# PEER experts: second products of four keys made in two stretches of four columns

## The reference

```python
experts = e1 * N_KEYS + e2                       # N_KEYS = 128
gate = softmax(top_s)
act = gelu(einsum('thkd,td->thk', expert_u[experts], tb)) * gate
out = einsum('thk,thkd->td', act, expert_v[experts])
```

## Time and profile before

| | us |
|---|---|
| median of 3 runs | 3780.93 (3779.2 to 3783.51) |
| the profiled execution | 3777.74 |
| its span | 3776.1 |
| TensorE matmul busy | 3400.2 (90%) |
| VectorE busy | 3066.7 (81%) |
| ScalarE busy | 1169.7 (31%) |
| GpSimd busy | 1518.2 (40%) |

### The profile page before, as it was taken

One profiled execution on the slowest core, in us unless ns is written; L12 is line 12 of the kernel. 1 busy time (PEld: TensorE's weight loads), 2 busy tenths in 40 slices (PEclk: granted clock), 3 DMA queues, 4 the chain that ended last, 5 costly groups with the idle time before them and its releaser, 6 DMA issues. The chain is left out here.

```text
span 3776.1 us, 64063 instructions
## 1 busy us (share of the span) xinstructions
PE 3400.2 (90%) x21871; PEld 3155.2 (84%) x21871; DVE 3066.7 (81%) x6071; ACT 1169.7 (31%) x2361; POOL 1518.2 (40%) x1267
## 2 busy tenths in 40 slices
PE   7998858989997998837779999999999999999997
PEld 7998747777786855537679999999999999999997
DVE  6543657676664589999879999999999999999997
ACT  3101344334232122249922222222222222222221
POOL 1120000000000023430067676676677766676772
PEclk9999769889898999969989999999999999999998
DMA  3222330010003000005499999999999999999995
GB/s 122 95 91 81 98 112 7 22 33 13 1 10 140 32 26 26 26 15 222 195 353 359 353 361 349 342 365 354 347 359 349 353 362 343 349 364 349 357 357 192
DMA packets 297939, 782.11 MB, mean 207 GB/s; under 512 B 28217, under 2 KB 130233, under 8 KB 296417
## 3 DMA queue, kind: packets, MB, share of 16 engines
q0 software_dynamic: 135568, 493.54, 35.5%
q1 hardware_dynamic: 162256, 287.15, 21.3%
HBM read 709.91 MB, written 70.11 MB: 207 GB/s over the span
## 5 line engine op out<-in xcount | busy, mean ns | idle before, releaser
L2982 POOL DMA_INDIRECT stream_u<-in_up_rows,experts_u_at x448 | 601.2, 1342 | 305.1 <-DVE experts_dot L3209 136.8
L2997 POOL DMA_INDIRECT stream_u<-in_down,experts_v_at x448 | 589.6, 1316 | 250.9 <-issue 97.7
L113 PE MATMUL experts_up_ps<-experts_u_hi,experts_up_hi 128*128 128x320 f32 x2048 | 635.8, 310 | 28.2 <-DVE experts_up_lo L3180 21.4
L113 PE MATMUL experts_down_ps<-experts_act_hi,experts_down_hi 128*128 128x320 f32 x2048 | 638.7, 312 | 12.5 <-DVE stream_h L3232 7.6
L115 PE MATMUL experts_up_ps<-experts_u_hi,experts_up_lo 128*128 128x320 f32 x2048 | 634.7, 310 | 0.8 <-issue 0.8
L114 PE MATMUL experts_down_ps<-experts_act_lo,experts_down_hi 128*128 128x320 f32 x2048 | 635.0, 310 | 0.2 <-issue 0.2
L115 PE MATMUL experts_down_ps<-experts_act_hi,experts_down_lo 128*128 128x320 f32 x2048 | 634.9, 310 | 0.0
L114 PE MATMUL experts_up_ps<-experts_u_lo,experts_up_hi 128*128 128x320 f32 x2048 | 634.9, 310 | 0.0
L3226 DVE SCALAR_TENSOR_TENSOR stream_h_rows_of<-stream_u,experts_weight,stream_h_rows_of 128x1024 f32<-128x1024 f32 x448 | 568.6, 1281 | 28.1 <-DMA stream_u<-in_down,experts_v_at 13.3
L3209 DVE CUSTOM_DVE_ANT_0 stream_u<-stream_u,stream_u_rows_of 128x1024 f32<-128x1024 f32 x448 | 545.8, 1218 | 38.3 <-DMA stream_u<-in_up_rows,experts_u_at 36.7
L113 PEld LDWEIGHTS experts_up_ps<-experts_u_hi,experts_up_hi 128*128 128x128 f32 x2048 | 386.3, 189 | 29.5 <-DVE experts_up_lo L3180 28.8
(11 more groups left out here) (453 smaller groups left out, 6346.4 us busy)
## 6 DMA issues: line engine op xcount, KB each, us to landing
stream_h_rest<-in_up SPq DMA_DIRECT2D x128, 512.0 KB, 4.5
stream_u<-in_down_pieces SPq DMA_DIRECT2D x128, 512.0 KB
gates<-spread_spread SPq DMA_DIRECT2D x10, 4096.0 KB, 11.5
experts_gates<-gates SPq DMA_DIRECT2D x64, 640.0 KB
cols<-inp_done POOLq DMA_DIRECT2D x26, 576.0 KB, 3.8
inp_w_in<-in_w_in SPq DMA_DIRECT2D x27, 512.0 KB, 4.4
pick_w_query<-in_w_query SPq DMA_DIRECT2D x14, 512.0 KB, 3.8
stream_u<-in_up_rows,experts_u_at POOLq DMA_INDIRECT x448
```

What stands on the lines that cost most here:

```text
L113: pe.matmul(out, w_hi, x_hi, start=start, stop=False)
L2982: pool.indirect_dma_start((half_row if i == HALF_DOT else u_row[b]), None, up_rows_d, bass.IndirectOffsetOnAxis(ap=u_at[slot][:, col:col + ...
L2997: pool.indirect_dma_start((half_row if i == HALF_ADD else v_row[b]), None, v_table, bass.IndirectOffsetOnAxis(ap=v_at[slot][:, col:col + 1 ...
```

## The change

TensorE makes the down product of quad q - 1 in two stretches: columns 0 to 3 behind up product 0 of quad q, as before, and columns 4 to 7 behind up product 1. The orders of ScalarE and VectorE are rearranged to suit: ScalarE does the gelu of key 1 and the rounding of up weight 3 ahead of the rounding of down piece 0 and the acts of keys 0 and 1; VectorE makes gate 1 and the split of up weight 3 ahead of column 4's sum, and the splits of down piece 0, of acts 0 and 1 and of down piece 1, and the sums of columns 5 to 7, later among the dots and adds. The order of dots and adds among themselves is unchanged. GpSimd's and SP's lists are unchanged.

```diff
--- before.py
+++ after.py
@@ -3057,9 +3057,9 @@
                                          u_hi[:, k, lo:lo + n], u_lo[:, k, lo:lo + n], k == 0, k == KD - 1)
                         mm.then_inc(up_done, 1)
 
-                def down_products(q):
+                def down_products(q, columns):
                     pe.wait_ge(act_split, FROM + q * QUAD_SIZE + QUAD_SIZE)
-                    for m in range(KD):
+                    for m in columns:
                         r, half = divmod(m, 2)
                         if half == 0:
                             pe.wait_ge(down_split, FROM + q * PIECES + (r + 1))
@@ -3075,10 +3075,14 @@
                     if has(q):
                         up_products(q, 0)
                     if has(q - 1):
-                        down_products(q - 1)
+                        down_products(q - 1, range(KD // 2))
                     if has(q):
-                        for e in range(1, QUAD_SIZE):
-                            up_products(q, e)
+                        up_products(q, 1)
+                    if has(q - 1):
+                        down_products(q - 1, range(KD // 2, KD))
+                    if has(q):
+                        up_products(q, 2)
+                        up_products(q, 3)
 
                 over_quads(pe, products)
                 pe.wait_ge(ones_ready, 1)
@@ -3143,14 +3147,14 @@
                         round_down(q - 1, 3)
                     if not has(q):
                         return
-                    round_down(q, 0)
-                    gelu_of_dots(q * 2, 0)
-                    round_act(q, 0)
-                    round_down(q, 1)
                     gelu(q, 1, 0)
                     gelu(q, 1, 1)
                     round_up(q, 3)
+                    gelu_of_dots(q * 2, 0)
+                    round_down(q, 0)
+                    round_act(q, 0)
                     round_act(q, 1)
+                    round_down(q, 1)
                     gelu(q, 2, 0)
                     gelu(q, 2, 1)
                     if has(q + 1):
@@ -3280,31 +3284,30 @@
                     if before:
                         split_down(q - 1, 3)
                     dots(0, 5)
-                    units(4)
                     adds(0, 4)
                     dots(0, 6)
+                    if now:
+                        gate(q, 1)
+                    adds(0, 5)
+                    if now:
+                        split_up(q, 3)
+                    units(4)
+                    adds(0, 6)
+                    dots(1, 0)
                     units(5)
-                    adds(0, 5)
-                    adds(0, 6)
-                    units(6)
+                    dots(1, 1)
                     if now:
                         split_down(q, 0)
-                    dots(1, 0)
+                    units(6)
+                    adds(1, 0)
+                    dots(1, 2)
+                    adds(1, 1)
                     units(7)
                     if now:
                         split_act(q, 0)
-                    dots(1, 1)
-                    adds(1, 0)
-                    if now:
+                        split_act(q, 1)
                         split_down(q, 1)
-                    dots(1, 2)
-                    adds(1, 1)
-                    if now:
-                        gate(q, 1)
                     dots(1, 3)
-                    if now:
-                        split_up(q, 3)
-                        split_act(q, 1)
                     adds(1, 2)
                     dots(1, 4)
                     adds(1, 3)
```

## The result

The changed kernel takes **3820.2 us** (3817.69 to 3822.43, four runs) against 3780.06 (3778.54 to 3783.51, four runs) for the kernel before: a ratio of 1.011, 95% interval 1.0094 to 1.0126, or 40 us more. The forecast was slower, 3808.5, range 3784 to 3850.

A forecast was written before the change was run, and what follows sets the result against it. A loop through TensorE and VectorE bounds the kernel: 57.30 + 0.45 + 0.15 = 57.90 us a round against 57.02, over thirty rounds 26.4, + 1.2 = 27.6, giving 3808.5 us, range 3784 to 3850.

The forecast's parts named there:

- VectorE's chain through E: From E, the first matmul after up product 1, through VectorE to column 2: 43.22 us, against TensorE's 42.25; loop 57.30.
- the 1 us named: Sign in the profile after: TensorE waits 1 us or more before column 2 in nearly every round.
- nowhere else: Sign in the profile after: TensorE waits before column 2 and at no other place.
- The bound given for being wrong: Row waits changing by more than 15 us in total, either way, would show the forecast wrong.
- I take that 0.45 for what it lacks: Allowance per round for VectorE's DMA row waits missing from the round shown: 0.45 us, bounds 0 to 1.05.
- The stretch of 33.89 us: Kernel before, from column 7's sum to the next sum of column 0 on VectorE; 26.93 us left after the change.
- the 0.15 for the clock: Allowance per round for clock falls and the fourth column's wait: 0.15 us, bounds 0 to 1.5.
- Rival (c): Bunched loads on the DMA engines add another 1 us of row waits a round behind column 7: 3838 us, chance 0.12.
- (a): VectorE's column waits shrink, row waits are absorbed, the loop falls to TensorE's 56.33 us: 3760 us, chance 0.08.
- (b): No change: row waits fall away as VectorE slows, rounds of 57.0 to 57.2 us: 3781 to 3788 us, chance 0.08.
- (d): TensorE's new waits lower its clock in most rounds, 0.95 to 2 us each: +45, 3854 us, chance 0.10.
- Start and end: First round's gain costed at nothing, bound 14.4 us; last down products' wait for the act split grows by about 1.2 us.

The follow-up runs named there:

- e3: Changed kernel with dot (1, 3) and add (1, 2) moved ahead of column 7's sum, the act splits and the split of down piece 1: 3785.99 us.
- e6: Changed kernel with SP's list alone altered, gates and up weight 5 loaded ahead of down piece 3: 3847.94 us, ratio 1.0174.
- e9: Kernel before with SP's list alone altered, gates and up weight 5 loaded ahead of down piece 3: 3820.67 us, ratio 1.0118.
- e8: Changed kernel with dot (1, 3) and add (1, 2) early, and gates and up weight 5 loaded ahead of down piece 3: 3779.63 us.
- e1: Kernel before with TensorE's two stretches alone, ScalarE's and VectorE's old orders kept: 3995.66 us, ratio 1.0567.
- e2: Changed kernel with add 5's row fetch put ahead of the half-row fetch in GpSimd's list: 3955.91 us, ratio 1.0451.

## Why the prediction was right, and where it was short

- **Direction and loop.** That VectorE's chain through E and not TensorE's work would set the round held: quiet rounds of 56.73 against TensorE's 56.33. The steps from E were met within 0.1 us (gate at 0.67, column 7's sum at 15.36). From there to the next sum of column 0 it is 27.67 us in the round shown, 26.23 without its waits (1.00 and 0.22 for rows, 0.22 for the product of weights); forecast were 26.93, or 26.27 without the 0.44 and 0.22 of such waits in it.
- **The signs.** The gate waits for ScalarE, columns 5 and 6 wait 0.35 us and column 7 does not, as written. The wait before column 2 is shorter than the 1 us named (21.3 us in 27), and wrong was "nowhere else": TensorE also waits at column 0, 34.0 us in 30, because the row wait of add (1, 5) lies ahead of the split of act 3 in VectorE's list; in e3 and e6, where add 5 does not wait, that wait is gone. The bound given for being wrong was met too: row waits grew by 31.5 us, over the 15 named.
- **The term that came out short** is "I take that 0.45 for what it lacks", the allowance for row waits. The stretch of 33.89 us that the loop was read from has 0.44 of such waits inside it, so the sum allowed 0.89 in all; measured were 2.10. The difference, 1.21 x 30 = 36 us, is more than the miss (56.5 against 27.6 forecast), because the loop without waits came out 0.13 lower than forecast and the 0.15 for the clock was hardly used (four falls in thirty rounds, two before).
- **Luck.** In the profiled pair 11.8 us of the 56.5 are hidden by a sooner start of the stage, and the medians differ by 40.1. With 56.5 on top of the median before, the time would have been 3837, inside the range to 3850 but outside the forecast's own 3788 to 3830.
- **Rival (c)** has the size of what happened and half of its mechanism: row waits of 0.9 to 1.05 us more a round, on the forecast's loop. It was priced at +1 and given 0.12. The text saw that three transfers that were spread would go out together while VectorE runs its chain, and then took the waits as they stood. The Trainium skill (DMA: Bandwidth & Descriptors, "Issuing engines are not separate DMA queues") says that transfers of different engines share the 16 DMA engines and interleave; the traces agree as far as they go: in the changed kernel add 5's row is used 8.94 us after its fetch with the loads together and at 7.34 without a wait with them apart (e6), in the kernel before 10.33 with them together (e9) and 8.26 apart.
- **What the prediction did not see** is GpSimd's list: the half-row fetch waits for dot (1, 3) and holds add 5's fetch. Before, the add asks 7.6 to 9.0 us after the fetch (8.04 on average), after 7.35. Add 5's wait grew from 0.22 to 1.59 us; 0.7 of the 1.37 is this shorter lead, and 0.7 the later landing. Those are readings of issue and use, not separate runs; e6 (landing) and e3 (both) each suffice to end this one wait. In the kernel's time only the early rows pay clearly (e3, and e8 against e6); with the loads apart alone the wait came back at dot (0, 2), which then asks 1.3 us sooner after its fetch.
- **Rivals (a) and (b)** fell: no row wait was absorbed. **(d)** fell as well for this kernel, with four clock falls; in e1 and e2 the clock falls in nearly every round.
- **Start and end.** From the first up product of the stage to the first sum of column 0 it is 69.3 us, 69.9 before: nothing gained, as costed. The last down products wait 4.8 us for the split of act in place of 3.68, and the tail grew by 1.5, 1.2 forecast.
- **The median** rose by 40.1 where the profiled pair differs by 44.7: the pair also contains earlier stages that ran 11.2 us shorter, and runs of the kernel before scattered from 3766 to 3795 us in the experiments.

## What to carry to other kernels

When three resources are near full, write down the loop through all engines twice, with and without the waits in the round that you read it from: once the loop passes the busiest engine's own time, every wait that used to vanish in the slack counts in full. When a step is moved, follow each in-order list that it gates (here SP's loads and GpSimd's fetches) and note which transfers now leave together and which fetch has less lead; equal bytes do not mean equal landing times. Two waits in one in-order list hide each other: with the first gone the second showed (e6), so test fixes together as well as alone. A change that loses may be worth a second try: here the gaps that it opened had to be filled and the loads moved apart before the kernel with it was the faster one.

## What the runs showed of the hardware that was not expected

- **A row fetch behind two or three bunched 512 to 640 KB loads** lands 2.4 us later in the rounds shown than in the same kernel with them apart (10.63 us after its issue, and by 8.21 us, e9 and before; 10.33 and by 8.26 over thirty rounds), for the same bytes a round.
- **Short waits on TensorE hardly touch the clock, longer ones mostly do.** After, the waits at column 0 are 1.1 us on average and those at column 2 0.8, and the granted clock fell to the lower level (0.5, 1.2 GHz) four times in thirty rounds, each time behind a single wait of 2.2 us or more (2.92, 2.22, 4.47, 2.33); two other such waits (3.02 and 2.27) and all of up to 1.96 us were not followed by a fall. In the kernel before it fell twice, behind the only two waits over 1 us (2.08 and 2.18). In e6 one wait of 2.5 us a round gave ten falls; in e1 3.9 us a round before an up product gave one in each round, and in e2 4.8 us a round gave 29.
- **An unchanged stage took 14 us less in one profile.** The same work ahead of the experts' stage, busy by stretch, in the kernel before:

```profile
480.00:1026.00 546.00, 454.64 (x2978) 379.08 (x2978) 349.48 (x762) 205.10 (x623) 12.27 (x20) 0.84 0.10 31
```

and after:

```profile
480.00:1012.00 532.00, 441.26 (x2972) 368.20 (x2971) 348.32 (x760) 203.91 (x617) 12.27 (x20) 0.86 0.10 31
```

VectorE and ScalarE work the same there within 1.2 us, TensorE is busy 13 us less at a granted clock of 0.86 instead of 0.84; the runs do not say why. Over the eleven profiles the first sum of column 0 in the experts' stage starts anywhere between 1947.7 us (after, the earliest) and 1962.7 (e2). It is a reason to compare stages by their own rows and not one span with another.
